# Two weight blocks at a time on two PSUM banks in the up and down stages of a four-layer float32 forward pass

## The reference

```python
def conv_ffn(h, w_up, conv_w, conv_b, w_down):
    u = causal_dwconv(h @ w_up, conv_w, conv_b)
    g, v = jnp.split(u, 2, axis=-1)
    return (jax.nn.gelu(g, approximate=True) * v) @ w_down

h = rmsnorm(x, ffn_norm[layer])
x = x + conv_ffn(h, ffn_w_up[layer], ffn_conv_w[layer], ffn_conv_b[layer], ffn_w_down[layer])
```

## Time and profile before

| | before |
|---|---|
| median of three runs | 3134.07 us |
| span of the profiled execution | 3131.4 us |
| TensorE busy | 3108.4 us, 99% |
| VectorE busy | 2315.0 us, 74% |
| ScalarE busy | 1650.6 us, 53% |
| transfers | 561.55 MB, 179 GB/s over the span |

### The profile page before, as it was taken

One profiled execution on the slowest core, in us unless ns is written; L12 is line 12 of the kernel. 1 busy time (PEld: TensorE's weight loads), 2 busy tenths in 40 slices (PEclk: granted clock), 3 DMA queues, 4 the chain that ended last, 5 costly groups with the idle time before them and its releaser, 6 DMA issues.

```text
span 3131.4 us, 52278 instructions
## 1 busy us (share of the span) xinstructions
PE 3108.4 (99%) x18922; PEld 2770.3 (88%) x18922; DVE 2315.0 (74%) x3605; ACT 1650.6 (53%) x2203; POOL 8.0 (0%) x12
## 2 busy tenths in 40 slices
PE   8999999999999999999999999999999999999998
PEld 7988888888888899988888888888898888888887
DVE  7877886787688778888866876878677777666665
ACT  5664554554455457755544544554446654444444
POOL 1000000000000000000000000000000000000000
PEclk9999999999999999999999999999999999999999
DMA  6335555555555645565555555555434455544443
GB/s 222 124 128 186 189 187 201 177 189 197 181 191 178 210 160 182 176 227 176 188 200 177 190 196 183 189 190 197 168 134 162 162 180 183 174 164 171 174 171 138
DMA packets 80334, 561.55 MB, mean 179 GB/s; under 512 B 9424, under 2 KB 10448, under 8 KB 13136
## 3 DMA queue, kind: packets, MB, share of 16 engines
q1 hardware_dynamic: 80208, 559.87, 51.2%
HBM read 557.73 MB, written 2.10 MB: 179 GB/s over the span
## 4 chain that ended last, share of the span: by engine, by line
PE 98%; DVE 1%; ACT 0%; DMA 0%; issue 0%; POOL 0%; DVEq 0%; SPq 0%; ACTq 0%
PE unit L317 50%; PE unit L320 26%; PE s L317 3%; PE s L320 1%; PE unit L540 1%; PE unit L590 1%; PE unit L592 1%; PE unit L591 1%; PE unit L542 1%; PE unit L541 1%; PE o L411 1%; PE tr L592 0%; PE tr L591 0%; PE tr L590 0%; PE unit L711 0%; PE v L317 0%
## 5 line engine op out<-in xcount | busy, mean ns | idle before, releaser
L1368 DVE TENSOR_TENSOR w_tail<-raw,w_head 128x2048 fp32r<-128x2048 f32 (+1 forms) x532 | 1207.5, 2271 | 140.0 <-ACT w_head L909 137.3
L909 ACT ACTIVATE w_head<-raw 128x2048 fp32r<-128x2048 f32 (+1 forms) x532 | 1011.2, 1901 | 496.1 <-DMA raw<-in_up 137.4
L317 PE MATMUL unit<-h,w_head 128*128 128x512 f32 x4912 | 1196.1, 392 | 0.0
L317 PEld LDWEIGHTS unit<-h,w_head 128*128 128x128 f32 x4912 | 902.8, 188 | 175.7
L320 PE MATMUL unit<-h,w_tail 128*128 128x256 f32 x4912 | 665.7, 284 | 0.0
L320 PEld LDWEIGHTS unit<-h,w_tail 128*128 128x128 f32 x4912 | 632.7, 191 | 18.4 <-issue 0.3
L1377 DVE TENSOR_TENSOR prod<-unit,lo 128x256 f32<-128x256 f32 x436 | 184.6, 423 | 391.3 <-ACT lo L916 389.4
L317 PE MATMUL unit<-act,w_head 128*128 128x512 f32 x1920 | 469.3, 391 | 0.0
L916 ACT ACTIVATE lo<-unit 128x256 f32<-128x256 f32 x436 | 166.8, 383 | 533.6 <-PE unit L320 518.5
L317 PEld LDWEIGHTS unit<-act,w_head 128*128 128x128 f32 x1920 | 353.2, 188 | 69.7
L320 PE MATMUL unit<-act,w_tail 128*128 128x256 f32 x1920 | 263.6, 283 | 0.0
(11 more groups left out here) (306 smaller groups left out, 2897.7 us busy)
## 6 DMA issues: line engine op xcount, KB each, us to landing
raw<-in_up SPq DMA_DIRECT2D x192, 1024.0 KB, 4.8
raw<-in_down SPq DMA_DIRECT2D x96, 1024.0 KB, 4.8
raw<-in_odd SPq DMA_DIRECT2D x64, 1024.0 KB, 4.8
raw<-in_even_b SPq DMA_DIRECT2D x32, 1024.0 KB, 4.8
raw<-in_attn SPq DMA_DIRECT2D x24, 1024.0 KB, 4.9
raw<-in_wo SPq DMA_DIRECT2D x16, 1024.0 KB, 4.8
raw<-in_lru_x SPq DMA_DIRECT2D x16, 1024.0 KB, 4.8
raw<-in_lru_y SPq DMA_DIRECT2D x16, 1024.0 KB, 4.8
```

The costliest lines, as they stand in the source:

```text
L317: pe.matmul(bank[:, :], w_head[:, slot, k * P:(k + 1) * P], src[:, k, :], start=k == 0, stop=False)
L909: a.activation(w_head[:, slot, 0:width], raw[:, r, 0:width], ACT.Copy).then_inc(head_done, 1)
L1368: v.tensor_tensor(w_tail[:, slot, 0:width], raw[:, slot % 2, 0:width], w_head[:, slot, 0:width].bitcast(F32), ALU.subtract).then_inc(tail_ ...
```

## The change

In the up and down stages TensorE takes two blocks at a time (`pair`): both blocks' rounded weights must be there; 32 heads, block and block by turns for each k, into two banks; then, when both rests are split, 32 rests by turns in the same way. The last rest of each block counts `unit_done`. The first two blocks of each such stage remain single. The banks go by turns over four (`score_bank`: unit0, unit1, s0, s1) in place of two, and a block or a pair waits for the bank's user four blocks before. ScalarE's and VectorE's code names the new banks, their order of work stays. The other stages keep `unit`.

```diff
--- before.py
+++ after.py
@@ -208,6 +208,7 @@
         ps_s = [ps_s0, ps_s1]
         score_bank = [*unit_bank, ps_s0, ps_s1]
         out_bank = {"wo": score_bank, "lru_out": wide_bank, "even_out": score_bank, "odd_out": score_bank}
+        out_bank.update((f"{kind}{layer}{r}", score_bank) for kind in ("up", "down") for layer in range(2) for r in range(ROUNDS))
 
         cst, cst_even, cst_gain, ones_in = sem("cst"), sem("cst_even"), sem("cst_gain"), sem("ones_in")
         x_in = [sem(f"x_in{c}") for c in range(4)]
@@ -412,12 +413,32 @@
                                      start=kt == 0, stop=kt == QT - 1)
                 last.then_inc(o_mm, 1)
 
+            def pair(u, slot, src):
+
+                pe.wait_ge(head_done, u + 2)
+                pe.wait_ge(bank_free, u + 1 - LEAD)
+                for k in range(KT):
+                    for s in range(2):
+                        pe.matmul(score_bank[slot + s][:, :], w_head[:, slot + s, k * P:(k + 1) * P], src[:, k, :],
+                                  start=k == 0, stop=False)
+                pe.wait_ge(tail_done, u + 2)
+                for k in range(KT):
+                    for s in range(2):
+                        last = pe.matmul(score_bank[slot + s][:, 0:SEQ], w_tail[:, slot + s, k * P:(k + 1) * P],
+                                         src[:, k, 0:SEQ], start=False, stop=k == KT - 1)
+                        if k == KT - 1:
+                            last.then_inc(unit_done, 1)
+
             def plain(name, src, ready=None, norm=None):
 
                 def body(i):
-                    for j in range(RING):
-                        first = known(i) and j == 0
-                        unit(i * RING + (BASE[name] + j), j, src, ready=ready if first else None, norm=norm if first else None)
+                    u = i * RING + BASE[name]
+                    if known(i):
+                        unit(u, 0, src, ready=ready, norm=norm, own=(score_bank[0], u - LEAD))
+                        unit(u + 1, 1, src, own=(score_bank[1], u + 1 - LEAD))
+                    else:
+                        pair(u, 0, src)
+                    pair(u + 2, 2, src)
                 repeat(pe, 0, UNITS[name] // RING, body)
 
             def residual(name):
@@ -1074,7 +1095,7 @@
             def up(name, layer, r):
                 def body(i):
                     for j in range(RING):
-                        step(i * RING + (BASE[name] + j), j, r == 0 and known(i) and i == 0 and j == 0)
+                        step(i * RING + (BASE[name] + j), j, r == 0 and known(i) and i == 0 and j == 0, bank=score_bank[j])
                         if j % 2:
                             a.wait_ge(gelu_in, i * 2 + (GELU_INS[name] + j // 2 + 1))
                             a.activation(kv[:, 5, :], kv[:, j, :], ACT.Gelu_apprx_tanh).then_inc(gelu_done, 1)
@@ -1624,7 +1645,7 @@
                     for j in range(RING):
                         u, c = i * RING + (BASE[name] + j), i * RING + (CONVS[name] + j)
                         last = final and j == RING - 1
-                        product(u, j)
+                        product(u, j, score_bank[j])
                         scaled(kv[:, 0, :]).then_inc(conv_in, 1)
                         if not last and not (r == 0 and known(i) and i == 0 and j == 0):
                             tail(u + LEAD, j + LEAD)
```

## The result

The changed kernel takes 3169.06 us (median of four runs, 3166.32 to 3169.84) against 3133.86 us for the kernel before: a ratio of 1.0111, 95% interval 1.0099 to 1.0123, or +35 us. The forecast was 3156, its own range 3150 to 3162, the wide range 3147 to 3174. The direction and the terms of the sum were right; rival B, TensorE's clock, came on top of it and accounts for the 13 us between. So the measured time lies outside the forecast's own range, and inside the wide one only because that took in B.

What follows compares the result with a forecast made beforehand. TensorE, busy 3108.4 of 3131.4 us, was taken to bound the kernel through matmul count times pitch plus standstills. The terms 19.8 + 5.0 - 2.6 = +22.2 us gave 3156 us, own range 3150 to 3162, wide range 3147 to 3174.

Steps and rivals of the forecast that it cites:

- rival B: TensorE's clock falls during the six hand-over standstills, 2.8 us each, 17 us in all, giving 3173 us; chance 0.13.
- Part 1, one switch less: In the 132 pairs, one switch from rests to heads instead of two saves 0.02 us each, 2.6 us gained.
- Part 2, banks in turn: In the pairs' heads and rests, alternating banks was taken to cost 0, between bounds of -8 and +21 us.
- Part 3 inside the stages: Both blocks' evacuations start together at a pair's end; 11.1 us of cover inside a stage hides them, cost 0.
- Rival C: The 0.5 us slack in up stages is missing as loads land late; a 0.2 us shortfall costs 17 us, 3173; chance 0.08.
- The hand-overs: At six up-to-down stage ends, k=15 waits for the late last act tile; TensorE stands 3.3 us each, 19.8 us.
- rival D: The stands are mostly covered because evacuations overlap more than chained; +5.7 us, 3140 us; chance 0.04.
- The norms: At the end of down02 and down12, TensorE stands 2.5 us for the norm's sum of squares, 5.0 us in all.
- The clock: The sum priced TensorE's stands at 3.3 and 2.5 us, with no clock fall added; a fall was left to rival B.

Runs made afterwards that it cites:

- folded pair: Changed kernel with pair order 16 heads of A, one of B, 16 rests of A, 16 rests of B, 15 heads of B; 3130.54 us, ratio 0.9991.
- two single blocks: Changed kernel with the last two blocks of each of the six up stages taken one after the other again; 3156.71 us, ratio 1.0078.
- run with five idle matmuls: Changed kernel with 5 extra heads into an unread bank before the wait for the last act tile in each down stage's first block; 3160.77 us.
- filled stands: Changed kernel with 13 extra heads into an unread bank before the wait for the last act tile in each down stage's first block; 3155.26 us, ratio 1.0069.
- heads by block: Changed kernel with the pair's 16 heads of block A before the 16 of block B, rests still in turn; 3169.39 us.
- rests by block: Changed kernel with the pair's 16 rests of block A before the 16 of block B, heads still in turn; 3140.90 us, ratio 1.0024.

## Why the prediction was right, and where it was off

- *Part 1, one switch less*, -2.6 us: right. A pair is 11.12 us against 2 x 5.57; the folded pair, which has this term and the four banks (no wait of the kernel before is for a bank), gained 3.0.
- *Part 2, banks in turn*, 0 within -8 to +21: right, and the bounds were far too wide; with and without turning the 32 heads last 7.44 us.
- *Part 3 inside the stages*, 0: right. The rounding that I placed at E+8.35 starts at 611.46, 8.4 us after the pair's end at 603.0. But the sentence that this costs nothing holds only in the stage: the late loads are a debt that comes due where pairs stop, as the two single blocks showed. Rival C (the 0.5 us of slack missing) did not come in the changed kernel: no wait for w_head stands in the list. But the slack is as thin as forecast: in the run with five idle matmuls one load of 6.0 us made a pair wait 0.7 us.
- *The hand-overs*, 6 x 3.3: right, and rival D (mostly covered) is out. TensorE's k=15 moved from 5.14 to 8.32 us after the pair's end, 3.2; six of them 19. The filled stands show the sum as a time: 3155.3 against the forecast 3156.3.
- *The norms*, 2 x 2.5: right in size. The profile has them as two idle gaps each. The first, 0.86, it puts down to no wait, but TensorE starts 0.11 us after the sum of block A, which frees the bank, ends at 1116.28; the second, 1.09, is for the sum of squares; the norm matmul starts at 1122.39, 6.86 us after the pair's end at 1115.53, against 4.52 in the earlier trace rows, 2.3.

```profile
1116.39 0.36 PE L611 MATMUL unit<-h,w_head 128*128 128x256 f32 x1 [0.86 <-issue]
...
1115.86 0.42 DVE L1398 TENSOR_TENSOR prod<-s,lo 128x256 f32<-128x256 f32 x1 [2.43 <-ACT lo L937]
...
1122.39 0.70 PE L360 MATMUL norm<-acc,ones 128*128 128x256 f32 x2 [1.09 <-DVE acc L1424]
```

- *The clock*: this step failed. The sum took each stand at its own length, and put the clock into rival B at 0.13. It fell at six of six. Its size was near: 2.8 us each forecast from the start of the kernel, 2.3 measured on average, 13.8 in place of 17; 3156 + 14 = 3170 is the time. That is partly luck, as the start is another case and the falls here cost 1.6 or 2.7 us. The gap of 1.51 us that it outlived was the only evidence, and it said nothing about twice that length. The Trainium skill (TensorE: Matmul & The Clock Gate, "HAM oscillation — how this bites in real kernels") names idle gaps between bursts as what puts the array to half clock; by that rule, the traces agree, at 3.0 us in 12 of 12 stands (the changed kernel and the one with heads by block). That gaps of 1.9 and 2.3 us can do it too the runs here show. I weighed the page too lightly against a row that did not reach the case.

## What to carry to other kernels

Work that is grouped to save on the bottleneck engine also groups what follows it; the cost doesn't show in the loop, where cover is plenty, but at its end, where the next stage wants the last result. Ask of every grouping when its first member is finished, and if the order can be folded so that it finishes as early as before. A stand of TensorE is to be priced with its clock: 3 us of idle time cost 5.5 here, and idle matmuls in the gap are worth it where the gap can't be closed.

## What the hardware showed that I had not expected

- No single length of idle gap decides on the clock. In the profiled executions, of six stands of 1.9 us three were followed by 1.2 GHz; of six of 2.0 to 2.5 us (two single blocks) one, of 2.3, while the longest two were not; of six of 1.2 us none. After stands of 3.0 us it fell every time, in some by the time TensorE resumed and in some a little over 1 us later.
- The changed kernel's runs spread over 3.5 us and those of the two single blocks over 8, while the kernel before and those with filled stands, rests by block and folded pairs, whose traces have no fall in the stages, stay within 1.1 us. That the number and kind of falls makes the spread is argued: the mean clock of the single-block runs goes from 0.998 for the fastest to 0.996 for the slowest, but only one of them has a trace.
- A head takes 0.227 us and a rest 0.120 from start to start at 2.4 GHz, whichever bank comes next. At 1.2 GHz, behind the stands, a head takes 0.427. Half of that is 0.213, so at the full clock 13 ns are added that the lower clock does not show. What they are stays open; the bank is excluded.
- Some loads of 1 MB take over 6 us in place of 4.8: 3 of 49 in the six stretches of 46 us above, and 10 to 15 of the 532 in each kernel's trace, the kernel before included. There they are covered. With a block's slack of 0.65 us, an estimate, it takes at least two blocks to make up for one.
